# Two blocks of one Trainium2 kernel joined more closely: raw blocks stored earlier, scan loads put ahead of small stores, the convolution loaded in four steps

## The reference, cut to what matters

```python
def mixer_block(h, lp, init, need_output):
    cb, cc, cx, r, k, v, w_lo, a_lo, g_lo = split_proj(h @ lp["w_in"])
    y, finals = rwkv_scans(r, k, v, w_lo, a_lo, lp, init)
    ...
    y_conv = cb * shortconv1d(cc * cx, lp["conv_a_w"])
    y_rwkv = rwkv_output(y, r, k, v, g_lo, lp)
    return jnp.concatenate([y_conv, y_rwkv], axis=-1) @ lp["w_out"], finals

def step(S, inp):                      # of wkv_scan, 8 heads of 64
    r_t, w_t, kk_t, b_t, v_t, k_t = inp
    sa = jnp.einsum("bhvk,bhk->bhv", S, kk_t)
    S = (S * w_t[:, :, None, :] - sa[..., None] * b_t[:, :, None, :]
         + v_t[..., None] * k_t[:, :, None, :])
    return S, jnp.einsum("bhvk,bhk->bhv", S, r_t)
```

## Time and profile before

| | us |
|---|---|
| median of 3 runs | 2266.69 |
| lowest, highest | 2255.43, 2269.16 |
| span of the profiled execution | 2265.7 |
| PE busy | 2050.2 (90%) |
| DVE busy | 1500.4 (66%) |
| ACT busy | 892.1 (39%) |
| POOL busy | 773.6 (34%) |

### The profile page before, as it was taken

One profiled execution on the slowest core, in us unless ns is written; L12 is line 12 of the kernel. 1 busy time (PEld: TensorE's weight loads), 2 busy tenths in 40 slices (PEclk: granted clock), 3 DMA queues, 4 the chain that ended last, 5 costly groups with the idle time before them and its releaser, 6 DMA issues. The chain is left out here.

```text
span 2265.7 us, 37012 instructions
## 1 busy us (share of the span) xinstructions
PE 2050.2 (90%) x15072; PEld 1594.0 (70%) x15072; DVE 1500.4 (66%) x2052; ACT 892.1 (39%) x1445; POOL 773.6 (34%) x460
## 2 busy tenths in 40 slices
PE   4989999837878898999999979999899999999898
PEld 1767677636767676788877768887677776776566
DVE  5777767679774548788988870454746676546644
ACT  5453443414434637333333331443434354333320
POOL 1144433300030145877777724533321111111111
PEclk7999999958899999999999999999999999999899
DMA  7535444597655422122221274523211111102512
GB/s 308 182 122 174 151 141 130 154 264 197 167 177 143 159 75 75 56 84 84 84 76 73 84 272 139 177 73 122 85 56 56 66 38 47 66 19 84 195 47 84
DMA packets 181335, 271.16 MB, mean 120 GB/s; under 512 B 74280, under 2 KB 122024, under 8 KB 176816
## 3 DMA queue, kind: packets, MB, share of 16 engines
q1 hardware_dynamic: 164816, 250.57, 33.9%
q10 hardware_dynamic: 16352, 18.22, 2.7%
HBM read 200.53 MB, written 68.23 MB: 119 GB/s over the span
## 5 line engine op out<-in xcount | busy, mean ns | idle before, releaser
L105 PE MATMUL b_ps<-h_hi,b_wpool 128*128 128x512 f32 (+1 forms) x896 | 277.4, 387 | 10.8 <-POOL b_wpool L744 10.8
L2995 PE MATMUL g_ps<-g_h_hi,w 128*128 128x512 f32 x784 | 260.0, 403 | 6.0 <-ACT g_q L3192 5.9
L3313 POOL TENSOR_TENSOR w<-raw_down,w 128x1024 fp32r<-128x1024 f32 x38 | 94.5, 2488 | 464.6 <-ACT w L3168 464.6
L2262 DVE SCALAR_TENSOR_TENSOR e_vars<-grid,vec,e_vars 128x1024 f32<-128x1024 f32 x168 | 216.0, 1285 | 7.4 <-ACT e_vars L2009 4.2
L105 PEld LDWEIGHTS b_ps<-h_hi,b_wpool 128*128 128x128 f32 x896 | 167.8, 192 | 56.3 <-POOL b_wpool L744 14.4
L2995 PEld LDWEIGHTS g_ps<-g_h_hi,w 128*128 128x128 f32 x784 | 149.3, 190 | 40.8 <-ACT g_q L3192 6.9
L105 PE MATMUL b_ps<-h_lo,b_wpool 128*128 128x512 f32 (+1 forms) x448 | 170.6, 381 | 0.0
L2995 PE MATMUL g_ps<-g_h_lo,w 128*128 128x512 f32 x392 | 156.1, 398 | 0.0
L2674 POOL TENSOR_TENSOR g_down_lo<-raw_down,g_down_hi 128x1408 fp32r<-128x1408 f32 x26 | 86.7, 3339 | 142.5 <-ACT g_down_hi L2574 142.5
L2513 PE MATMUL g_pb<-g_z_hi,g_down_hi 128*128 128x512 f32 x286 | 114.8, 401 | 14.7 <-DVE g_down_lo L2751 9.8
L744 POOL TENSOR_TENSOR b_wpool<-raw_in,b_wpool 128x1024 fp32r<-128x1024 f32 x26 | 67.9, 2611 | 173.2 <-ACT b_wpool L530 173.2
(11 more groups left out here) (524 smaller groups left out, 5284.4 us busy)
## 6 DMA issues: line engine op xcount, KB each, us to landing
e_raw_up<-w_ffn SPq DMA_DIRECT2D x22, 1024.0 KB, 4.9
raw_down<-w_down SPq DMA_DIRECT2D x32, 704.0 KB, 4.2
c_op<-ops SPq DMA_DIRECT2D x40, 512.0 KB, 5.0
raw_down<-w SPq DMA_DIRECT2D x38, 512.0 KB, 3.7
raw_in<-w SPq DMA_DIRECT2D x26, 512.0 KB, 4.2
mod_stage<-ada_rows ACTq DMA_DIRECT2D x24, 512.0 KB, 3.7
zs<-e_z SPq DMA_DIRECT2D x21, 512.0 KB, 2.6
ops<-b_xin SPq DMA_DIRECT2D x20, 512.0 KB, 4.7
```

The lines of the kernel that those rows point to most:

```text
L105: last = nc.tensor.matmul(out, w[:, k, :], x[:, k, cols], start=(k == 0 and n == 0), stop=(k == nk - 1 and n == 2))
L2262: STT(out=acc, in0=view, scalar=wt, in1=acc, op0=ALU.mult, op1=ALU.add).then_inc(sem("conv"), 1)
L2995: mm = nc.tensor.matmul(out_bank, ww[w % 2][:, k], xx[g][:, k], start=(k == 0 and a == 0), stop=(k == KD - 1 and a == 2))
L3313: nc.gpsimd.tensor_tensor(w_lo[w % 2], raw[:, w % 2], w_hi[w % 2].bitcast(F32), ALU.subtract).then_inc(sem("lo"), 1)
```

## The change

What it does, in order of the program:

1. **Raw blocks of batch 0.** ACT copies the first pair of raw blocks before its last `powers`, not after. The 16 stores to `pb[0]` are split: SP issues eight after `store_job(3, 4)` and four after `store_job(3, 5)`; ACT issues the last four.
2. **The end of projections.** The closing waits of SP for its stores are gone; their semaphores are now of the outer set, and the scan waits for them where it reads. SP now loads `nb` for batch 0 before the barrier, after a wait for all 16 raw stores, and only then stores the last convolution chunk.
3. **Memory.** `nb` and `ui` lie in the place of `mod_stage` and `c_silu`. POOL clears `ui` at the end of projections and `ti` at the start of the scan; DVE's three memsets at the start of the scan are gone.
4. **The scan's prologue.** `load_blocks(0)` is gone; `load_blocks(1)`, which waits for the raw stores of batch 1, now stands ahead of `store_blocks(0)`.
5. **Steps 0, 3 and 7** load slot s + 3 for both directions ahead of `store_raw`; the steps after them load none.
6. **The convolution** is loaded one chunk a step in steps 10 to 13.

```diff
+        def store_raw(eng, i, dirs):
+            for x in dirs:
+                eng.wait_ge(sem(f"raw_blocks{x}"), i + 1)
+                for h in range(2):
+                    for b in range(2):
+                        eng.dma_start(d["pb"][0, x, h, b, ...], pre[x][i][...]).then_inc(t["ahead"]("pb_first"), 16)
...
             store_job(m, 4)
+            store_raw(sp, 0, (0, 1))
             store_job(m, 5)
-            sp.dma_start(d["pends"], t["pend"][:, 1, NCTX:SLOTS]).then_inc(sem("pend"), 16)
+            store_raw(sp, 1, (0,))
+            sp.dma_start(d["pends"], t["pend"][:, 1, NCTX:SLOTS]).then_inc(t["ahead"]("pends_stored"), 16)
+            sp.wait_ge(t["ahead"]("pb_first"), 256)
+            sp.wait_ge(sem("mod_used"), MODS)
+            sp.dma_start(t["nb"][:, 0:(C // 2) ** 2], d["pb"][0]...).then_inc(t["ahead"]("nb_first"), 16)
             store_conv(m)
-            sp.wait_ge(sem("pb"), 256)
-            sp.wait_ge(sem("pend"), 16)
-            sp.wait_ge(sem("sg_stored"), 16)
-            for j in range(2):
-                sp.wait_ge(sem(f"ops_stored{j}"), 16 * (1 + j) * NJ // 2 * PAIRS)
-            sp.wait_ge(sem("vt_stored"), 128 * PAIRS)
-            sp.wait_ge(sem("bonus_stored"), 16 * PAIRS)
-            sp.wait_ge(sem("conv_stored"), 16 * PAIRS)
...
             read_cc(c, 2)
+            raw_blocks(0)
             powers(m, 5)
-            (copies and 16 stores of the raw blocks)
+            raw_blocks(1)
+            store_raw(act, 1, (1,))
...
+            pool.wait_ge(sem("mod_used"), MODS)
+            nc.gpsimd.memset(t["ui"], 0.0).then_inc(sem("ui_zero"), 1)
+            pool.wait_ge(sem("ui_zero"), 1)
+            nc.gpsimd.memset(t["ui"][:, 0:(C // 2) ** 2:C // 2 + 1], 1.0).then_inc(t["ahead"]("ui_clear"), 1)
...
+            def raw_in(s):
+                return s == 0 or s in pres and pres[s] % 2 == 1
+
             def step(s):
                 for x in DIRS:
-                    if s + 2 < STEPS:
+                    if s + 2 < STEPS and not raw_in(s - 1):
                         load(x, s + 2)
+                for x in DIRS:
+                    if s + 3 < STEPS and raw_in(s):
+                        load(x, s + 3)
                 if s == 0:
                     store_raw(2)
...
-                if s == 10:
-                    load_conv()
+                if 10 <= s < 10 + KD // 2:
+                    load_conv([s - 10])
...
-            load_blocks(0)
+            for x in DIRS:
+                sp.wait_ge(t["ahead"](f"ops_stored{x}"), OPS_STORED[x])
+            sp.wait_ge(t["ahead"]("vt_stored"), 128 * PAIRS)
             for x in DIRS:
                 load(x, 0)
...
             sp.wait_ge(sem("clear"), 4)
+            load_blocks(1)
             store_blocks(0)
-            load_blocks(1)
...
-            nc.vector.memset(ti[:], 0.0).then_inc(sem("ui_clear"), 1)
-            nc.vector.memset(ui[:], 0.0).then_inc(sem("ui_clear"), 1)
-            dve.wait_ge(sem("ui_clear"), 2)
-            nc.vector.memset(ui[:, 0:HB * HB:HB + 1], 1.0).then_inc(sem("ui_clear"), 1)
-            dve.wait_ge(sem("ui_clear"), 3)
+            dve.wait_ge(t["ahead"]("ui_clear"), 1)
             for part in range(4):
                 blocks(0, part)
...
         def _(pool):
+            nc.gpsimd.memset(ti[:], 0.0).then_inc(sem("ti_clear"), 1)
+            for x in DIRS:
+                pool.wait_ge(t["ahead"](f"ops_stored{x}"), OPS_STORED[x])
```

More of the change, by code:

```diff
@@ L274, in _ @@
             sp.wait_ge(sem("read_a"), act_read[("g", 0, 2)])
-            sp.dma_start(d["sgs"], sq[:, 0:SEQ]).then_inc(sem("sg_stored"), 16)
+            sp.dma_start(d["sgs"], sq[:, 0:SEQ]).then_inc(t["ahead"]("sg_stored"), 16)
             load_w(("r", 0))
@@ L303, in _ @@
             for j in range(2):
-                sp.wait_ge(sem(f"ops_stored{j}"), 16 * (1 + j) * (NJ // 2 * m + 1))
+                sp.wait_ge(t["ahead"](f"ops_stored{j}"), 16 * (1 + j) * (NJ // 2 * m + 1))
             for i in range(2):
@@ L561, in read_vt @@
                 if n:
-                    act.wait_ge(sem("vt_stored"), n * 128)
+                    act.wait_ge(t["ahead"]("vt_stored"), n * 128)
                 A(vt[:, at // P:(at + m) // P].rearrange("p j c -> p (j c)"), ps[PS_HEADS][:, 0:m], ACT.Copy).then_inc(sem("vt"), 1)
@@ L609, in inputs_hi, with raw_blocks @@
                       bias=t["mod"][:, c, kt:kt + 1]).then_inc(sem("h_hi"), 1)
+            def raw_blocks(i):
+                for x in range(2):
+                    act.wait_ge(sem(f"p_blocks{x}"), i + 1)
+                    A(pre[x][i][:, :, 0:C], block_bank[x][:].rearrange("p (n c) -> p n c", c=C), ACT.Copy).then_inc(sem(f"raw_blocks{x}"), 1)
             act.wait_ge(sem("vecs"), 16)
@@ L855, in keys @@
                 elif g == 0:
-                    dve.wait_ge(sem("sg_stored"), 16)
+                    dve.wait_ge(t["ahead"]("sg_stored"), 16)
                 TS(kk[:, cols(g)], k[:, cols(g)], k_k[:, n:n + 1], None, ALU.mult).then_inc(sem("kk_raw"), 1)
@@ L872, in products_rk @@
                 if n:
-                    dve.wait_ge(sem("bonus_stored"), n * 16)
+                    dve.wait_ge(t["ahead"]("bonus_stored"), n * 16)
                 STT(out=rkk, in0=r[:, CTX:TOK], scalar=r_k[:, n:n + 1], in1=k[:, CTX:TOK], op0=ALU.mult,
@@ L888, in conv_taps @@
                 if c:
-                    dve.wait_ge(sem("conv_stored"), c * 16)
+                    dve.wait_ge(t["ahead"]("conv_stored"), c * 16)
                 dve.wait_ge(sem("u"), 2 * c + 2)
@@ L1127, in load_w1, with load_conv @@
                 sp.dma_start(w1_raw[:, n % 2], d["w_out"][n // 2][:, n % 2, 0:KD // 2]).then_inc(done, 16)
-            def load_conv():
-                for k in range(KD // 2):
+            def load_conv(part):
+                for name in ("conv_stored", "bonus_stored"):
+                    sp.wait_ge(t["ahead"](name), 16 * PAIRS)
+                sp.wait_ge(t["ahead"]("sg_stored"), 16)
+                for k in part:
                     sp.dma_start(hc[:, k, 1].bitcast(F32), d["mixd"][:, k]).then_inc(sem(f"hc{k}"), 16)
@@ L1204, in _ @@
                 load(x, 1)
+            sp.wait_ge(t["ahead"]("pends_stored"), 16)
             for h in HEADS:
@@ L1523, in blocks @@
                 if part == 0:
-                    dve.wait_ge(sem("nb"), 16 * (T + 1))
                     if T:
+                        dve.wait_ge(sem("nb"), 16 * T)
                         dve.wait_ge(sem("ub"), 16 * T)
+                    else:
+                        dve.wait_ge(t["ahead"]("nb_first"), 16)
                     diag = lambda buf: buf[:, 1:HB * HB:2 * (HB + 1)]
@@ L1535, in blocks @@
                         dve.wait_ge(sem("tb"), 16 * T)
+                    else:
+                        dve.wait_ge(sem("ti_clear"), 1)
                     for row in (0, 8):
@@ L3578, in program @@
         with ExitStack() as first:
-            t["mod_stage"], t["c_silu"] = keep(first, "mod_stage", [P, 2, D]), keep(first, "c_silu", [P, D])
+            rows = keep(first, "mod_stage", [P, 3 * D])
+            t["mod_stage"], t["c_silu"] = rows[:, 0:2 * D].rearrange("p (s d) -> p s d", s=2), rows[:, 2 * D:3 * D]
+            t["nb"], t["ui"] = (rows[:, n * (C // 2) * (C // 2 + 1):(n + 1) * (C // 2) * (C // 2 + 1)] for n in range(2))
         t["sq_hi"], t["headones_r"] = keep(whole, "sq_hi", [P, 2, SEQ], F32R), keep(whole, "headones_r", [P, P], F32R)
```

33 lines of the change are left out of this document (12 added, 21 removed).

## The result

| | before | after |
|---|---|---|
| median of 16 runs, us | 2267.81 | 2274.82 |
| lowest, highest, us | 2255.43, 2277.61 | 2269.44, 2283.04 |
| span of the profiled execution, us | 2265.7 | 2272.0 |

The ratio is 1.0033 with a 95% interval of 1.002 to 1.0047: the change costs about 7 us, where 6 us less were forecast. It lies outside the range of 2250 to 2271.

What follows compares the result with a forecast made beforehand. It took stores, loads and a serial DVE inversion at the border of projections and scan, then two long scan steps, to bound the kernel; 2 + 1.5 + 3 - 1.5 + 1 = 6.0 us faster gave 2260.5, range 2250 to 2271.

Steps and rivals of the forecast that it cites:

- the end of projections: Raw stores shared between SP and ACT before the barrier: scan starts 1.7 us earlier to 2.7 later, 1 earlier taken.
- something not seen here: What a slowdown of 1% (22.7 us) would need; chance 0.02.
- `nb` 1 ahead of the stores: Scan's prologue: `ui` store leaves 2.0 us earlier, `nb` ahead costs 1.9; first step gains 0 to 2.
- SP's single list becomes the gate: Rival, scan's prologue: `ui` and `ti` stores wait behind late raw stores of batch 1; 3.5 us slower, 2270; chance 0.12.
- SP's list and the start of the scan: Before the barrier: SP's list takes 13.0 to 17.4 us, ending at 456.7 to 461.1; scan starts 1 us earlier.
- `nb` before the barrier: Start of the scan: batch 0's `nb` there at 459.9 against 463.35, 3.4 us for DVE.
- the whole border: Projections to scan, all border parts together: 2 us gained, ends -2 and +4.
- Loads ahead: Steps 3 and 7: loads use a 22% busy stretch, PE's issue gap shrinks; 1.5 us gained, ends 0 and 4.
- sign of being wrong: Named in advance: the forecast is wrong if the issue gaps turn up elsewhere at the same total.
- Convolution in four steps: Step 10: three loads leave, 3 us gained, ends 0 and 5; slot 16's load later, 1.5 charged.
- Hidden anyway: Rival: PE's gaps move to the next full queue; only 0 to 3 us remain, about 2265.5; chance 0.20.
- POOL beside DVE: Steps 11 to 13: spreading POOL's pairs returns 1 of 2.1 us on DVE's path, ends -1 and 2.

Runs made afterwards that it cites:

- e1: Changed kernel with its ten new outer semaphores numbered before anything else, work and waits the same; 2268.97 us, ratio 1.0018.
- e2: Kernel before, with the semaphores of its eight closing waits taken from the outer set at first use; 2272.99 us, ratio 1.0026.
- e9: Kernel before plus ten unused outer semaphores, taken at every seventh of the projections' own; 2274.59 us, ratio 1.0034.
- e10: e2 with its eight outer semaphores numbered first; 2268.35 us, ratio 0.9998 to the kernel before.
- e6: e4 with the four convolution chunks loaded together in step 10 again; 2262.43 us, ratio 0.9976 to the kernel before.
- e8: e4 with all nineteen outer semaphores numbered first; 2261.61 us, ratio 0.9986 to the kernel before.
- e12: e6 with all nineteen outer semaphores numbered first; 2267.36 us, ratio 1.0004 to the kernel before.
- e5: e4 with the loads of steps 0, 3 and 7 put back behind the raw stores; 2266.97 us, ratio 0.9993.
- e4: Changed kernel, its ten new outer semaphores numbered first and batch 0's `ui`/`ti` stores ahead of batch 1's `nb` load; 2262.8 us, ratio 0.9988.
- e3: Changed kernel with batch 0's `ui` and `ti` stores put back ahead of batch 1's `nb` load; 2273.12 us, ratio 1.0026.

## Why the prediction was wrong

**The step that failed is the one that isn't there.** Among the parts, the end of projections was priced by SP's list alone, and the move of its semaphores to the outer set got no term at all: 0 instead of the 6.2 us that the traces show. e1 takes these out of the changed kernel (5.9 us by the medians, 4.7 +- 4.5 by the means), e2 and e9 put them into the kernel before (5.8 and 7.7; 4.9 +- 4.1 and 7.4 +- 2.5), e10 takes them out again. The size is that of the traces; the runs bear it out to some 3 us. The kernel before had the sign of it. It clears 1, 2, 3 and 13 ranges, and its closings take 0.98, 1.06, 1.35 and 3.41 us, growing with the outer semaphores taken so far. The view that shows it is the idle time that ends with L83, read at each barrier and not only at the one that the diff touches. The "something not seen here" of the prediction is a rule of the allocator and four barriers.

**`nb` 1 ahead of the stores** was seen and mis-sized. The wait itself did no harm: raw stores landed at 487.01, `ub`'s store left 28.95 us after the scan's start, as before. The queue cost was priced at 1.9 us and was 2.6 on SP's read-back and 3.0 on ACT's. The gain set against it was mostly not there: DVE got `nb` 1 only 2.6 us earlier on the clock (492.71), not over 4, and gave that back in the wait of 4.09 us, which the prediction had named as a possibility and not charged. The first step was to gain 0 to 2 us; it lost 1.1 for the first direction and 3.0 for the second (503.52 against 500.54, which the prediction took for the begin of the step; that was 498.45). Counted from DVE's last product of projections, which leaves out that this execution's projections ended earlier, the first `chain_s` comes 5.2 us later than before, 1.3 of it by the clearing. The prediction's window for PE's first blocks, 499 to 500.5, was met by the first direction alone. The rival "SP's single list becomes the gate" has the right place and sign, but the wrong condition: it was to need late raw stores, and the 512 KB alone did it.

**SP's list and the start of the scan.** Terms right: 12 raw stores took 10.95 us (8.2 to 12.0), the two of job 5 1.26 (1.4 to 2.0), `pends` 0.45 instead of 2.25. The barrier is reached 6.3 to 6.6 us after DVE's last product in the kernels with the new border and 6.6 to 6.9 with the old one: 0.3 us won where 1 was taken. The scan's first load at 458.56 lies in the named window of 457 to 460, but only because this execution's projections ended 2.3 us earlier; the clearing ate 1.3 us of it.

**`nb` before the barrier** held: DVE's first instruction of batch 0 at 459.40, named 459 to 461. Counted from its last product of projections, DVE starts batch 0 at 9.8 us instead of 11.5, where 3.4 us were hoped for. What is left of it at the first `chain_s`, with the stores first, is 1 to 2 us. Forecast for the whole border were 2.

**Loads ahead.** In this profile the gap of 3.57 us in step 4 shrank to 0.83, with another of 2.23 behind it, and step 4 to 5 fell to 13.2, below the 16 named. That fall is real: 16.5 to 12.3 in the mean of seven profiles each, with no overlap. Most of it is a term that the prediction hadn't: PE's mean granted clock in this step is 0.67 to 0.81 without the loads ahead and 0.87 to 1.00 with them, and PE is busy for 12.6 us of the step against 9.5. So about 3 of the 4.2 us are the same products at a faster clock (before, it was at 0.53 from 568.0 to 572.5, around the gap). The room that the prediction saw was used: in the stretch that was 22% full, the engines now work at 85% (windows, after):

```profile
548.00:552.00 4.00, 4.00 (x73) 3.54 (x70) 2.02 (x3) 1.11 (x5) 0.00 (x0) 0.50 0.85 265
```

The stretch lies in another part of the step now, so this is no comparison like for like; and PE worked through it at half clock. But the time isn't saved: 2.1 us of it are lost in step 3 to 4 and 2.0 in steps 5 to 10, and steps 2 to 10 take the same. The prediction's own sign of being wrong came true, that the gaps turn up elsewhere at the same total: PE's issue gaps of 0.3 us and more in steps 0 to 19 sum to 13 to 20 us (mean 16.7) in the seven profiles without the loads ahead and 13 to 21 (mean 17.5) in the seven with them; e1, e6, e8 and e12 have one of 3.4 to 3.7 us in step 3. The step that failed here is the last one, from a shorter step to a shorter scan. e5 against e4 leaves 0 for the term, its lower end.

**Convolution in four steps.** Failed: 3 us were taken, 0 came. Step 10 to 11 is at 15.6, above the 14 named; the issue gap grew from 2.57 to 3.40 though three of four loads had left the step. Much of the step's excess was chance: with all four loads in it, it takes 12.9 to 16.4 us in eight profiles, with one 13.0 to 15.6 in six (means 14.7 and 14.3). Steps 10 to 12 gain 1.9 us in the mean and steps 12 to 17 lose 2.5. My inference that PE's own instructions are late behind that data gets no support; what makes the gaps stays open. Slot 16's wait came out at 1.49 after 1.43, where up to 1.9 us more were charged. e6, with all four loads at once again, is the lowest ratio of all. "Hidden anyway" was the right case for both edits of the steps.

**POOL beside DVE.** In the after profile POOL works at 652.57 to 656.06 and 668.19 to 671.73, and step 11 to 12 takes 667.28 - 656.03 = 11.25 us instead of 14.2. The collision of the earlier trace rows did go from this step of this profile. But e4 and e5, with the same loads, take 14.2 and 14.3 us there, and in e4 POOL works at 653.46 to 656.99 and 664.43 to 667.90, inside the step: where POOL meets DVE changes with the execution. In the mean step 11 to 12 takes 13.3 us with the convolution in four steps and 14.8 without, near the 1 us taken, and it is among what steps 12 to 17 give back. What this is worth alone was not tried.

**Sum.** 6.2 (ranges) + 4 (`nb` ahead; the mean of 1.7 by the changed kernel and e3 and 6.2 by e1 and e4) - 2.5 (all else, e4 to e8 and e12) = 7.7, where 7.0 were measured by the medians and 7.6 by the means. The forecast had 0, a charge inside its 2, and -6. The last two terms are known only to 2 or 3 us each, so that the sum comes out so well is luck; the sign and the largest term don't hang on it.

## What to carry to other kernels

Before a semaphore, a buffer or any other numbered thing is given a longer life, ask who pays when the short-lived ones around it are given back; number the long-lived first. Read the idle time at every barrier, not only at the one that the diff touches, and compare whole spans with the sum of those: a loss that no stage shows may lie between the stages. A long step in one profile may be that execution's alone, and a step made shorter is worth nothing until the stretch up to the next fixed point is shorter too: several profiles, compared by stretch, show it where 12 runs can't. A small transfer for which the critical path waits belongs ahead of a large one on its queue, even where the issue costs nothing.

## What the runs showed of the hardware

GpSimd needs 0.16 us for each further contiguous range of semaphores that it clears (40 ranges: 6.2 us; 28: 4.4 us), and in this kernel every engine waits for it. A range's length matters less: clearing all semaphores of the projections as one range took 0.50 us, as ten ranges 0.80 us without what lies between them.

DVE and POOL block each other more widely than the one pair of the earlier trace rows. In the kernel before, DVE's instruction on eight elements beside an arithmetic one of POOL, and the same alone, each with its successor:

```profile
439.66 1.25 DVE L840 TENSOR_SCALAR pend<-b_xin 128x8 f32<-128x8 f32 x1
440.82 0.68 DVE L842 TENSOR_TENSOR b_xin<-b_tmp,b_xin 128x512 f32<-128x512 f32 x1
...
444.66 0.17 DVE L840 TENSOR_SCALAR pend<-b_xin 128x8 f32<-128x8 f32 x1
444.74 0.68 DVE L842 TENSOR_TENSOR b_xin<-b_tmp,b_xin 128x512 f32<-128x512 f32 x1
```

```profile
439.14 1.72 POOL L759 TENSOR_TENSOR b_xin<-b_xin,b_tmp 128x512 f32<-128x512 f32 x1
```

It takes 0.17 us alone and 1.25 beside POOL; it ends at 440.91, when POOL's ends at 440.86, and DVE goes on 1.16 us after its start instead of 0.08.
```profile
437.37 2.17 DVE L846 TENSOR_SCALAR pend<-b_xin 128x8 f32<-128x8 f32 x1
438.53 1.01 DVE L848 TENSOR_TENSOR b_xin<-b_tmp,b_xin 128x512 f32<-128x512 f32 x1
```

```profile
438.53 0.98 POOL L796 MEMSET mod_stage<- 128x1056 f32 x1
...
458.48 0.98 POOL L1602 MEMSET c_ti<- 128x1056 f32 x1 [18.76 <-POOLq L83]
459.40 1.88 POOL L1607 MEMSET c_ud<- 128x1024 f32 x2
```

The first of them cost DVE nothing: the small instruction is listed with 2.17 us, but its successor still begins 1.16 us after it, and in e1, with the same memset, it takes 1.25. Those on `ti` and `ud` did cost: beside them the first instruction on `nb` takes 0.99 instead of 0.31. So of the cover on POOL some 0.7 us were paid on DVE.

PE's granted clock at the end of the scan differs from one execution to the next. Its level was 1.00 from 745 to 760 in the profile of the kernel before. After, it fell to half (1.2 GHz) in a stretch in which PE worked 3.11 of 5 us (before, it kept its level there with 3.32), and stayed there across the barrier:

```profile
740.00:745.00 5.00, 3.11 (x99) 2.85 (x96) 0.48 (x2) 2.22 (x7) 0.00 (x0) 0.84 0.01 3
745.00:750.00 5.00, 3.34 (x70) 2.87 (x67) 2.05 (x5) 0.00 (x0) 0.00 (x0) 0.50 0.01 3
753.00:756.00 3.00, 3.00 (x5) 1.01 (x3) 0.00 (x0) 0.00 (x0) 0.00 (x0) 0.50 0.86 235
```

Its first four products of `mix_up` take 3.75 us instead of 1.95, and so they do in e1, whose barrier is as short as before; e9, with the long barrier, has 2.45. This is one execution each. It moves a profile by 1.8 us in these four products alone, and it is one reason why none of the sums above rests on the two spans alone.
